# Retention: one written-out pipeline over all heads in place of a loop over head pairs

## The chip, the cores and the metric

The kernel runs on one core of one Trainium2 chip. The metric is the device time of one execution in microseconds (us), as the median of several runs. Engines are called PE (TensorE matmul), PEld (its weight loads, which overlap PE), DVE (VectorE), ACT (ScalarE), POOL (GpSimd) and SP (SyncE, which here only issues DMAs).

## What is computed

The kernel computes two layers of a decoder trunk on 1024 tokens of width 1024, all in float32. The change touches one stage of the second layer, the retention mixer, with 8 heads, key width 128, value width 256 and chunks of 128 tokens:

```python
def retention_mixer(h, positions, w_in, gn_g, gn_b, w_out):
    proj = h @ w_in                       # 1024 x (8*128 + 8*128 + 8*256 + 8*256)
    q, k, v, gate = jnp.split(proj, ...)
    q = apply_rope(q, cos, sin) * (RET_DK ** -0.5);  k = apply_rope(k, cos, sin)
    o = chunkwise_retention(q, k, v)
    o = layer_norm(o, gn_g, gn_b)         # per head
    return (jax.nn.silu(gate) * o) @ w_out
# chunkwise_retention, for each head and chunk i, with the head's decay powers:
#   inner = (q_i k_i^T * decay) v_i ;  cross = (q_i state) * cross_decay
#   state = state * chunk_decay + (k_i * key_decay)^T v_i
```

Heads are independent of one another. Within a head the chunks are chained by the state.

## The kernel before

`layer_1` runs its stages one after another, each in a block of its own that ends with a barrier of all engines: `modulate` (writes `g.hT`, the transposed input), `retention` (writes `mixT`), `mix_out` (the output projection) and then the mixture of experts.

In `retention` a step is one chunk of 128 tokens of one head. The weight panel of a head, `w[u]` (1024 rows by 768 columns, 3 MB), comes by four DMAs from SP (L1762). There are two such buffers, u = 0 and 1. A loop over `pairs` = 4 head pairs runs on every engine (`Fori`), and its body is 16 steps written out (`STEPS`): head 2m in `w[0]`, then head 2m+1 in `w[1]`.

The body is a software pipeline. In slot s PE issues, in this order, `project(s)` (q, k, v of the chunk: 8 matmuls of 512 columns, L1805), `output(s-2)` (L1834, L1836, L1837; without L1836 for the first chunk of a head), `turn(s-1)` (two transposes, L1821), `project_gate(s)` (8 matmuls of 256 columns, L1813), `score(s-1)` (L1827) and `turn_back(s-3)` (two transposes, L1844). A float32 matmul stands in the profile as two records. Since the body begins at s = 0 and runs to s = STEPS + 2, the pipeline is filled at the start of each pair and emptied at its end: slots 16, 17 and 18 of the body have only what is left of steps 13 to 15.

Behind PE, ACT takes q, k and v out of PSUM (`take`, L1879, L1881), makes the reciprocal root (`root`, L1894 and L1896, each with a table load), takes the turned q and k (`take_turned`, L1901), the gate (`take_gate`, L1888) and the turned result (`take_back`, L1907, into `mixT`). DVE ropes q and k (L1942 to L1947), masks the scores (L1952), updates the state, takes the moments (L1960 to L1966) and centres the output (L1971). POOL multiplies by the gain, adds the bias and multiplies by the gate (L1790, L1792, L1794); it reads `head_gain` and `head_bias`, copies of the pair's rows that it makes at the top of each pass (L1784, L1785).

All waits count from the start of the stage: `before(m, s)` and `after(m, s)` add `m * STEPS`, so inside the loop each wait compares a semaphore with a value worked out from the loop's register. SP waits at the top of pass m, for both panels, until all 16 gate projections of pass m-1 are done (`sp.wait_ge(S["gates"], m * STEPS)`).

Of the kernel before, what the change touches and what calls it, by code (L numbers as in the profile page):

```python
# [17 lines left out]
P = 128  # L18
D = 1024
T = 1024  # L20
NT = T // P
# [1681 lines left out]
def retention(g, mixT):  # L1703
    nc, io = g.nc, g.io
    STEPS = 2 * NT
# [4 lines left out]
    with ExitStack() as ctx:  # L1710
# [21 lines left out]
        head_gain = [sb(f"head_gain{u}", [P, RDV]) for u in range(2)]  # L1732
        head_bias = [sb(f"head_bias{u}", [P, RDV]) for u in range(2)]
# [6 lines left out]
        names = ("rows placed rates exps qkv gates taken gated roped turned turnc scored masked out moments logs roots norms rowsc "  # L1740
# [7 lines left out]
        for width in (RDK, RDK, RDV, RDV):  # L1748
            cols = w_dram[:, :, at:at + HEADS * width].rearrange("p k (m u n) -> p k m u n", u=2, n=width)
            parts.append((off, width, cols))  # L1750
            at += HEADS * width
            off += width
        pairs = HEADS // 2

        before = lambda m, s: m * STEPS + max(s, 0)
        after = lambda m, s: m * STEPS + s + 1

        @block.sync
        def _(sp):
            def panel(m, u):  # L1760
                for off, width, cols in parts:
                    sp.dma_start(w[u][:, :, off:off + width], cols[:, :, bass.ds(m, 1), u, :]  # L1762
                                 .rearrange("p k a n -> p k (a n)")).then_inc(w_in[u], 16)

            with sp.Fori(0, pairs) as m:
                for u in range(2):

                    sp.wait_ge(S["gates"], m * STEPS)
                    panel(m, u)

        @block.gpsimd
        def _(pool):
            pool.iota(place_i[:, :], [[1, 1]], base=1, channel_multiplier=1).then_inc(S["placed"], 1)
            for h in range(HEADS):
                pool.memset(rate[:, 0, h:h + 1], lg[h]).then_inc(S["placed"], 1)
                pool.memset(rate[:, 1, h:h + 1], -lg[h]).then_inc(S["placed"], 1)
                pool.memset(chunk_decay[:, h:h + 1], math.exp(RDK * lg[h])).then_inc(S["placed"], 1)
            pool.wait_ge(S["rows"], 32)
            gp = gain[:, :, :].rearrange("p (m u) n -> p m u n", u=2)
            bp = bias[:, :, :].rearrange("p (m u) n -> p m u n", u=2)  # L1780
            with pool.Fori(0, pairs) as m:
                for u in range(2):
                    row = lambda t: t[:, bass.ds(m, 1), u, :].rearrange("p a n -> p (a n)")
                    pool.tensor_copy(head_gain[u][:, :], row(gp)).then_inc(S["rowsc"], 1)  # L1784
                    pool.tensor_copy(head_bias[u][:, :], row(bp)).then_inc(S["rowsc"], 1)  # L1785
                for s in range(STEPS):
                    u, zb = s // NT, z[s % 4][:, :]
                    pool.wait_ge(S["norms"], after(m, s))
                    pool.wait_ge(S["rowsc"], m * 4 + 4)
                    pool.tensor_tensor(zb, zb, head_gain[u][:, :], ALU.mult).then_inc(S["gained"], 1)  # L1790
                    pool.wait_ge(S["gained"], m * 3 * STEPS + 3 * s + 1)
                    pool.tensor_tensor(zb, zb, head_bias[u][:, :], ALU.add).then_inc(S["gained"], 1)  # L1792
                    pool.wait_ge(S["gained"], m * 3 * STEPS + 3 * s + 2)
                    pool.tensor_tensor(zb, zb, gate[s % 4][:, :], ALU.mult).then_inc(S["gained"], 1)  # L1794

        @block.tensor
        def _(pe):
            with pe.Fori(0, pairs) as m:
                def project(s):
                    u, t = s // NT, s % NT  # L1800
                    if t == 0:
                        pe.wait_ge(w_in[u], m * 64 + 64)
                    pe.wait_ge(S["taken"], before(m, s - 1))
                    for kk in range(KD):
                        mm = pe.matmul(p_qkv[s % 2][:, :], g.hT[:, kk, t * P:(t + 1) * P], w[u][:, kk, 0:512],  # L1805
                                       start=(kk == 0), stop=(kk == KD - 1))
                    mm.then_inc(S["qkv"], 1)

                def project_gate(s):
                    u, t = s // NT, s % NT  # L1810
                    pe.wait_ge(S["gated"], before(m, s - 1))
                    for kk in range(KD):
                        mm = pe.matmul(p_gate[s % 2][:, 0:RDV], g.hT[:, kk, t * P:(t + 1) * P], w[u][:, kk, 512:W],  # L1813
                                       start=(kk == 0), stop=(kk == KD - 1))
                    mm.then_inc(S["gates"], 1)

                def turn(s):
                    pe.wait_ge(S["roped"], m * 6 * STEPS + 6 * s + 6)
                    pe.wait_ge(S["turnc"], before(m, s))
                    for i in range(2):  # L1820
                        mm = pe.transpose(p_turn[:, i * P:(i + 1) * P], qkr[s % 4][:, i, :], g.ident[:, :])  # L1821
                    mm.then_inc(S["turned"], 1)

                def score(s):
                    pe.wait_ge(S["turnc"], after(m, s))
                    pe.wait_ge(S["masked"], before(m, s))
                    pe.matmul(p_scores[:, 0:P], qkT[s % 2][:, 1, :], qkT[s % 2][:, 0, :], start=True, stop=True)\  # L1827
                        .then_inc(S["scored"], 1)

                def output(s):  # L1830
                    t = s % NT
                    pe.wait_ge(S["masked"], after(m, s))
                    pe.wait_ge(S["norms"], before(m, s))
                    pe.matmul(p_out[:, 0:RDV], scores[s % 2][:, :], v[s % 4][:, :], start=True, stop=(t == 0))  # L1834
                    if t:
                        pe.matmul(p_out[:, 0:RDV], qkT[s % 2][:, 0, :], state[(s - 1) % 2][:, :], start=False, stop=True)  # L1836
                    pe.matmul(p_out[:, RDV:2 * RDV], qkr[s % 4][:, 1, :], v[s % 4][:, :], start=True, stop=True)\  # L1837
                        .then_inc(S["out"], 1)

                def turn_back(s):  # L1840
                    pe.wait_ge(S["gained"], m * 3 * STEPS + 3 * s + 3)
                    pe.wait_ge(S["backc"], before(m, s))
                    for i in range(2):
                        mm = pe.transpose(p_back[:, i * P:(i + 1) * P], z[s % 4][:, i * P:(i + 1) * P], g.ident[:, :])  # L1844
                    mm.then_inc(S["back"], 1)

                for s in range(STEPS + 3):
                    if s < STEPS:
                        project(s)
                    if 0 <= s - 2 < STEPS:  # L1850
                        output(s - 2)
                    if 0 <= s - 1 < STEPS:
                        turn(s - 1)
                    if s < STEPS:
                        project_gate(s)
                    if 0 <= s - 1 < STEPS:
                        score(s - 1)
                    if 0 <= s - 3 < STEPS:
                        turn_back(s - 3)

        @block.scalar
        def _(act):
# [7 lines left out]
            dp = decay[:, :, :].rearrange("p i (m u) -> p i m u", u=2)  # L1870
            mp = mixT[:, :, :].rearrange("p (m k) t -> p m k t", k=4)
            with act.Fori(0, pairs) as m:
                def take(s):
                    u, b = s // NT, s % 4
                    act.wait_ge(S["qkv"], after(m, s))
                    act.wait_ge(S["roped"], m * 6 * STEPS + max(6 * (s - 1), 0))

                    act.wait_ge(S["out"], before(m, s - 3))
                    act.copy(v[b][:, :], p_qkv[s % 2][:, QK:512])  # L1879
                    for i in range(2):  # L1880
                        ins = act.activation(qk[s % 2][:, i, :], p_qkv[s % 2][:, i * RDK:(i + 1) * RDK], ACT.Copy,  # L1881
                                             scale=dp[:, i, bass.ds(m, 1), u])
                    ins.then_inc(S["taken"], 1)

                def take_gate(s):
                    act.wait_ge(S["gates"], after(m, s))
                    act.wait_ge(S["gained"], m * 3 * STEPS + max(3 * (s - 3), 0))
                    act.activation(gate[s % 4][:, :], p_gate[s % 2][:, 0:RDV], ACT.Silu).then_inc(S["gated"], 1)  # L1888

                def root(s):  # L1890
# [791 lines left out]
```

## Time and profile before

| | |
|---|---|
| median of 3 runs | 3802.49 us |
| lowest and highest of them | 3797.62, 3807.16 us |
| the profiled execution | 3790.52 us |
| its span, first to last instruction | 3788.7 us |
| PE busy over the span | 3229.5 us (85%) |
| ACT, DVE, POOL busy | 24%, 34%, 13% |
| retention, first projection to last transpose | 1923.52 to 2770.99 us of the span |

A timeline row has the start, the duration, the engine, the line, the operation with its output and inputs, the count of merged records, and in brackets how long the engine sat idle before it and what ended that. Ends of matmuls are modelled and overlap a little, so durations on PE are best read as the distance between the starts of two rows. A row of windows gives for a stretch its length, then for each engine the busy us and the number of instructions, then the granted TensorE clock as a share of full speed, the DMA share and GB/s.

### The profile page before, as it was taken

How to read it: one execution, taken by the hardware profiler on the slowest of the kernel's cores; microseconds unless marked ns; L12 is line 12 of the kernel's file. 1: busy time of each engine (PE TensorE's matmuls, PEld its weight loads, DVE VectorE, ACT ScalarE, POOL GpSimd, SP SyncE). 2: the span in 40 equal slices, each digit the busy share in tenths (PEclk: the TensorE clock that was granted, in tenths of full speed). 3: DMA queues.
4: the chain of work that ended last, by engine and by line, in shares of the span. 5: the costliest groups of instructions: out<-in, count | busy, mean ns of one | idle time of the engine just before them, and what ended most of it. 6: DMA issues, size and time to landing. Idle time of an engine off the chain costs nothing. (4 is left out here: it accounts for less than half of the span.)

```text
span 3788.7 us, 44646 instructions
## 1 busy us (share of the span) xinstructions
PE 3229.5 (85%) x15035; PEld 1782.1 (47%) x15036; DVE 1274.6 (34%) x3073; ACT 908.2 (24%) x1749; POOL 503.7 (13%) x866
## 2 busy tenths in 40 slices
PE   7978889677865999999479899999989759988884
PEld 5656654367434434333146565655644343433331
DVE  4665554354243112221623232232311241121226
ACT  1022224123120111111135354453410011111111
POOL 0000010166010000000301111111100100000003
PEclk9879999778885999999689999999989859999997
DMA  7722001122235999996530202010030157899985
GB/s 283 270 87 84 0 23 34 49 65 47 89 104 230 388 367 411 425 426 236 214 111 1 67 0 67 0 45 22 0 122 34 60 230 300 329 427 424 426 358 200
DMA packets 195570, 668.26 MB, mean 176 GB/s; under 512 B 46863, under 2 KB 97770, under 8 KB 162414
## 3 DMA queue, kind: packets, MB, share of 16 engines
q1 hardware_dynamic: 162574, 579.56, 39.5%
q0 software_dynamic: 14144, 51.39, 3.5%
q10 hardware_dynamic: 18720, 35.66, 2.5%
q8 instruction: 70, 1.15, 0.1%
q14 instruction: 62, 0.51, 0.0%
HBM read 605.17 MB, written 61.37 MB: 176 GB/s over the span
## 5 line engine op out<-in xcount | busy, mean ns | idle before, releaser
L1805 PE MATMUL ret_pqkv<-ret_w,hT_mix 128*128 128x512 f32 x1024 | 457.6, 600 | 20.0 <-DMA ret_w<-in_ret_w_in_dram 20.0
L2354 PE MATMUL f0e_pgu<-f0w_gu,f0e_xT 128*64 128x512 f32 x1568 | 344.8, 596 | 7.0 <-issue 3.2
L1678 PE MATMUL mo_py<-mo_w,mixT 128*128 128x512 f32 x768 | 333.4, 597 | 4.8 <-DMA mo_w<-in_ret_w_out_dram 2.5
L1805 PEld LDWEIGHTS ret_pqkv<-ret_w,hT_mix 128*128 128x128 f32 x1024 | 192.6, 193 | 240.1 <-issue 239.9
L2354 PE MATMUL f1e_pgu<-f1w_gu,f1e_xT 128*64 128x512 f32 x1344 | 296.0, 595 | 7.4 <-issue 3.6
L1678 PEld LDWEIGHTS mo_py<-mo_w,mixT 128*128 128x128 f32 x768 | 147.0, 192 | 192.6 <-issue 184.8
L1813 PE MATMUL ret_pgate<-ret_w,hT_mix 128*128 128x256 f32 x1024 | 231.6, 379 | 0.0
L2354 PEld LDWEIGHTS f0e_pgu<-f0w_gu,f0e_xT 128*64 128x64 f32 x1568 | 125.4, 138 | 220.9 <-issue 220.8
L2373 PE MATMUL f1e_pd<-f1w_d,f1e_hidT 128*64 128x512 f32 x672 | 173.1, 668 | 52.6 <-DMA f1w_d<-in_moe_w_down_dram 51.3
L1813 PEld LDWEIGHTS ret_pgate<-ret_w,hT_mix 128*128 128x128 f32 x1024 | 189.9, 190 | 25.0 <-issue 1.9
L2354 PEld LDWEIGHTS f1e_pgu<-f1w_gu,f1e_xT 128*64 128x64 f32 x1344 | 104.2, 138 | 194.1 <-issue 194.0
L2373 PE MATMUL f0e_pd<-f0w_d,f0e_hidT 128*64 128x512 f32 x784 | 176.9, 600 | 7.4 <-DMA f0w_d<-in_moe_w_down_dram 5.5
L434 PE MATMUL gc_pq<-hT_mix,gc_w 128*128 128x512 f32 x384 | 168.3, 597 | 10.1 <-DMA gc_w<-in_hy_w_in_dram 10.1
L1960 DVE TENSOR_TENSOR ret_state<-ret_state,ret_pout 128x256 f32<-128x256 f32 x56 | 23.5, 421 | 406.2 <-PE ret_pout L1837 406.2
L2502 DVE COPY f0e_hidT<-f0e_ph 128x512 f32<-128x512 f32 x32 | 22.1, 691 | 363.7 <-PE f0e_ph L2366 363.3
L2502 DVE COPY f1e_hidT<-f1e_ph 128x512 f32<-128x512 f32 x32 | 22.1, 691 | 359.0 <-PE f1e_ph L2366 359.0
L1790 POOL TENSOR_TENSOR ret_z<-ret_z,ret_head_gain 128x256 f32<-128x256 f32 x64 | 46.5, 726 | 700.5 <-DVE ret_z L1971 700.5
L2373 PEld LDWEIGHTS f1e_pd<-f1w_d,f1e_hidT 128*64 128x64 f32 x672 | 53.0, 153 | 149.4 <-issue 93.5
L434 PEld LDWEIGHTS gc_pq<-hT_mix,gc_w 128*128 128x128 f32 x384 | 73.4, 192 | 102.3 <-issue 91.9
L1879 ACT COPY ret_v<-ret_pqkv 128x256 f32<-128x256 f32 x64 | 23.8, 372 | 389.1 <-PE ret_pqkv L1805 389.1
L1598 DVE TENSOR_TENSOR mo_z<-mo_py,mo_gate_b 128x1024 f32<-128x1024 f32 x16 | 19.6, 1225 | 272.0 <-PE mo_py L1678 272.0
L2373 PEld LDWEIGHTS f0e_pd<-f0w_d,f0e_hidT 128*64 128x64 f32 x784 | 58.3, 138 | 102.7 <-issue 94.2
(547 smaller groups left out, 4705.4 us busy)
## 6 DMA issues: line engine op xcount, KB each, us to landing
f0w_gu<-in_moe_w_gate_dram SPq DMA_DIRECT2D x32, 2048.0 KB, 11.3
f0w_gu<-in_moe_w_up_dram SPq DMA_DIRECT2D x32, 2048.0 KB, 16.8
f0w_d<-in_moe_w_down_dram SPq DMA_DIRECT2D x64, 1024.0 KB, 15.8
f1w_gu<-in_moe_w_gate_dram SPq DMA_DIRECT2D x32, 2048.0 KB, 25.5
f1w_gu<-in_moe_w_up_dram SPq DMA_DIRECT2D x32, 2048.0 KB, 30.5
f1w_d<-in_moe_w_down_dram SPq DMA_DIRECT2D x64, 1024.0 KB, 24.9
mixT<-in_ada_w_dram SPq DMA_DIRECT2D x80, 512.0 KB, 5.6
expert_rows<-f0e_y ACTq DMA_DIRECT2D x64, 256.0 KB, 10.4
```

The lines of the kernel that those rows point to most:

```text
L434: mm = pe.matmul(pq[u][:, half * 512:(half + 1) * 512], w[u][:, kk, :], g.hT[:, kk, half * 512:(half + 1) * 512], start=(kk == 0), stop=(k ...
L1598: dve.tensor_tensor(z[:, :], y, self.gate_b[:, :], ALU.mult).then_inc(S["zmul"], 1)
L1678: mm = pe.matmul(py[t % 3][:, half * 512:(half + 1) * 512], mixT[:, kk, t * P:(t + 1) * P], ws[:, kk, half * 512:(half + 1) * 512], start= ...
L1790: pool.tensor_tensor(zb, zb, head_gain[u][:, :], ALU.mult).then_inc(S["gained"], 1)
L1805: mm = pe.matmul(p_qkv[s % 2][:, :], g.hT[:, kk, t * P:(t + 1) * P], w[u][:, kk, 0:512], start=(kk == 0), stop=(kk == KD - 1))
L1813: mm = pe.matmul(p_gate[s % 2][:, 0:RDV], g.hT[:, kk, t * P:(t + 1) * P], w[u][:, kk, 512:W], start=(kk == 0), stop=(kk == KD - 1))
L1879: act.copy(v[b][:, :], p_qkv[s % 2][:, QK:512])
L1960: ch.mark(dve.tensor_tensor(st[:, :], state[(s - 1) % 2][:, :], p_out[:, RDV:2 * RDV], ALU.add))
L2354: mm = pe.matmul(pgu[s][half * HALF:(half + 1) * HALF, :], xT[u % 2][:, kk, s * HALF:(s + 1) * HALF], ew.gu[u][:, :, kk, half * FH:(half + ...
L2373: mm = pe.matmul(pd[s][half * HALF:(half + 1) * HALF, :], hidT[:, s, k % 2, k // 2, :], ew.d[u % 2][:, k, half * DH:(half + 1) * DH], star ...
L2502: dve.tensor_copy(hidT[:, :, :, :, :].rearrange("p s j h t -> p (s j h t)"), ph[:, :])\
```

## The change

The loop over pairs is gone on all engines. `STEPS` is now 64, all eight heads, written out once; the pipeline is filled at step 0 of head 0 and emptied after step 63. Every wait compares with a constant. Head h uses `w[h % 2]`. SP loads the panel of head h as soon as the gates of head h-2 are done, the head that had the same buffer. `head_gain` and `head_bias`, their copies and the semaphore `rowsc` are gone, POOL reads `gain[:, h, :]` and `bias[:, h, :]`. The order of the operations within a slot, the number of buffers and all operations on PE, ACT and DVE stay as they are.

```diff
-    STEPS = 2 * NT
+    STEPS = HEADS * NT
...
-        head_gain = [sb(f"head_gain{u}", [P, RDV]) for u in range(2)]
-        head_bias = [sb(f"head_bias{u}", [P, RDV]) for u in range(2)]
...
-        before = lambda m, s: m * STEPS + max(s, 0)
-        after = lambda m, s: m * STEPS + s + 1
+        before = lambda s: max(s, 0)
+        after = lambda s: s + 1
...
-            with sp.Fori(0, pairs) as m:
-                for u in range(2):
-
-                    sp.wait_ge(S["gates"], m * STEPS)
-                    panel(m, u)
+            for h in range(HEADS):
+                if h >= 2:
+                    sp.wait_ge(S["gates"], (h - 1) * NT)
                 for off, width, cols in parts:
+                    sp.dma_start(w[h % 2][:, :, off:off + width], cols[:, :, h, :]).then_inc(w_in[h % 2], 16)
...
-            with pool.Fori(0, pairs) as m:
-                for u in range(2):
-                    row = lambda t: t[:, bass.ds(m, 1), u, :].rearrange("p a n -> p (a n)")
-                    pool.tensor_copy(head_gain[u][:, :], row(gp)).then_inc(S["rowsc"], 1)
-                    pool.tensor_copy(head_bias[u][:, :], row(bp)).then_inc(S["rowsc"], 1)
-                for s in range(STEPS):
-                    pool.wait_ge(S["rowsc"], m * 4 + 4)
-                    pool.tensor_tensor(zb, zb, head_gain[u][:, :], ALU.mult).then_inc(S["gained"], 1)
+            for s in range(STEPS):
+                h, zb = s // NT, z[s % 4][:, :]
+                pool.tensor_tensor(zb, zb, gain[:, h, :], ALU.mult).then_inc(S["gained"], 1)
...
-            with pe.Fori(0, pairs) as m:
-                def project(s):
-                    u, t = s // NT, s % NT
-                    if t == 0:
-                        pe.wait_ge(w_in[u], m * 64 + 64)
-                    pe.wait_ge(S["taken"], before(m, s - 1))
+            def project(s):
+                h, t = s // NT, s % NT
+                if t == 0:
+                    pe.wait_ge(w_in[h % 2], 64 * (h // 2 + 1))
+                pe.wait_ge(S["taken"], before(s - 1))
...
```

The other functions of the five engines change in the same way: `before(m, s)` to `before(s)`, slices by `bass.ds(m, 1)` to slices by h.

## Rows read from the trace of the kernel before

**Rows 1.** PE timeline: the first projection of each of the four passes
```profile
1923.52 9.16 PE L1805 MATMUL ret_pqkv<-ret_w,hT_mix 128*128 128x512 f32 x16 [20.04 <-DMA ret_w<-in_ret_w_in_dram]
...
2135.67 8.90 PE L1805 MATMUL ret_pqkv<-ret_w,hT_mix 128*128 128x512 f32 x16
...
2347.46 4.96 PE L1805 MATMUL ret_pqkv<-ret_w,hT_mix 128*128 128x512 f32 x7
...
2559.17 5.34 PE L1805 MATMUL ret_pqkv<-ret_w,hT_mix 128*128 128x512 f32 x8
```

**Rows 2.** Windows: steps 3 to 14 of passes 0 and 1
```profile
1958.60:2107.10 148.50, 148.50 (x528) 92.64 (x527) 45.25 (x157) 72.44 (x132) 26.27 (x37) 1.00 0.00 1
2170.49:2319.01 148.52, 148.52 (x529) 92.64 (x527) 45.30 (x158) 72.46 (x132) 26.28 (x37) 1.00 0.00 0
```

**Rows 3.** Windows: step 10, with a head's first output, and step 11
```profile
2045.41:2057.50 12.09, 12.09 (x45) 7.37 (x44) 3.86 (x14) 6.19 (x12) 2.09 (x4) 1.00 0.01 2
2057.50:2069.90 12.40, 12.40 (x47) 7.75 (x45) 3.77 (x14) 5.94 (x12) 2.26 (x4) 1.00 0.00 1
```

**Rows 4.** PE timeline: the end of pass 0, from output(14) on
```profile
2119.84 0.70 PE L1834 MATMUL ret_pout<-ret_v,ret_scores 128*128 128x256 f32 x2 [0.17 <-DVE ret_scores L1952]
...
2124.93 0.49 PE L1827 MATMUL ret_pscores<-ret_qkT 128*128 128x128 f32 x2 [3.31 <-ACT ret_qkT L1901]
...
2125.80 1.22 PE L1834 MATMUL ret_pout<-ret_v,ret_scores 128*128 128x256 f32 x2 [0.16 <-DVE ret_scores L1952]
...
2134.98 0.69 PE L1844 MATMUL ret_pback<-ident,ret_z 128*128 128x128 f32 x2 [5.83 <-POOL ret_z L1794]
```

**Rows 5.** PE timeline: the end of pass 3
```profile
2755.10 0.70 PE L1834 MATMUL ret_pout<-ret_v,ret_scores 128*128 128x256 f32 x2 [0.17 <-DVE ret_scores L1952]
...
2770.30 0.69 PE L1844 MATMUL ret_pback<-ident,ret_z 128*128 128x128 f32 x2 [6.04 <-POOL ret_z L1794]
2774.89 3.78 PE L1572 MATMUL mo_py<-mo_diag,ones 128*128 128x512 f32 x4 [3.89 <-DVE mo_diag L1565]
```

**Rows 6.** Windows: the gap between passes 0 and 1
```profile
2119.84:2135.67 15.83, 6.53 (x22) 4.40 (x23) 4.09 (x13) 8.13 (x14) 6.80 (x12) 0.79 1.05 308
```

**Rows 7.** SP timeline: the panel loads at the start and after pass 0
```profile
1906.62 18.45 SPq L1762 DMA_DIRECT2D ret_w<-in_ret_w_in_dram  x8
...
2119.27 14.55 SPq L1762 DMA_DIRECT2D ret_w<-in_ret_w_in_dram  x8
```

**Rows 8.** DMA view, 2131 to 2152: GB/s in 40 equal slices of 0.525 us
```profile
GB/s 295 295 287 295 287 311 342 345 363 332 312 343 353 351 355 334 205 74 59 6 0 0 0 0 0 0 0 0 0 0 0 0 0 0 0 0 0 0 0 0
```

**Rows 9.** ACT timeline: `take_back` under a panel load, and in the steady part
```profile
2125.76 0.37 ACT L1907 COPY mixT<-ret_pback 128x256 f32 x1 [0.88 <-PE ret_pback L1844]
...
2246.18 0.37 ACT L1907 COPY mixT<-ret_pback 128x256 f32 x1
```

**Rows 10.** DMA view, passes 0 (1923 to 2134) and 1 (2152 to 2346): instruction queues
```profile
q8 instruction: 6, 0.10, 0.2%
q14 instruction: 5, 0.04, 0.1%
...
q14 instruction: 3, 0.02, 0.0%
```

**Rows 11.** Windows: the longest stretch at full granted clock, in the experts
```profile
1231.90:1576.64 344.74, 337.37 (x1638) 137.87 (x1636) 63.99 (x152) 53.38 (x133) 21.86 (x38) 1.00 0.96 395
```

**Rows 12.** PE timeline: gate, and what follows the score, in step 1 and steadily
```profile
2154.95 3.62 PE L1813 MATMUL ret_pgate<-ret_w,hT_mix 128*128 128x256 f32 x16
...
2158.62 1.88 PE L1805 MATMUL ret_pqkv<-ret_w,hT_mix 128*128 128x512 f32 x4
...
2253.29 3.62 PE L1813 MATMUL ret_pgate<-ret_w,hT_mix 128*128 128x256 f32 x16
...
2257.09 0.38 PE L1844 MATMUL ret_pback<-ident,ret_z 128*128 128x128 f32 x2
```

More of the change, by code:

```diff
@@ L1739, in retention @@
         p_back = g.ps(ctx, "ret_pback", [P, 512])
-        names = ("rows placed rates exps qkv gates taken gated roped turned turnc scored masked out moments logs roots norms rowsc "
+        names = ("rows placed rates exps qkv gates taken gated roped turned turnc scored masked out moments logs roots norms "
                  "gained back backc").split()
@@ L1748, in retention @@
         for width in (RDK, RDK, RDV, RDV):
[L1749 removed]
+            cols = w_dram[:, :, at:at + HEADS * width].rearrange("p k (h n) -> p k h n", n=width)
             parts.append((off, width, cols))
@@ L1796, in _ @@
         @block.tensor
         def _(pe):
-            with pe.Fori(0, pairs) as m:
-                def project(s):
-                    u, t = s // NT, s % NT
-                    if t == 0:
-                        pe.wait_ge(w_in[u], m * 64 + 64)
-                    pe.wait_ge(S["taken"], before(m, s - 1))
[L1804 to L1859, printed above, removed]
@@ new lines, in project, with project_gate @@
+            def project(s):
[3 more added lines that the diff above has]
+                pe.wait_ge(S["taken"], before(s - 1))
+                for kk in range(KD):
+                    mm = pe.matmul(p_qkv[s % 2][:, :], g.hT[:, kk, t * P:(t + 1) * P], w[h % 2][:, kk, 0:512],
+                                   start=(kk == 0), stop=(kk == KD - 1))
+                mm.then_inc(S["qkv"], 1)
+            def project_gate(s):
+                h, t = s // NT, s % NT
+                pe.wait_ge(S["gated"], before(s - 1))
+                for kk in range(KD):
+                    mm = pe.matmul(p_gate[s % 2][:, 0:RDV], g.hT[:, kk, t * P:(t + 1) * P], w[h % 2][:, kk, 512:W],
+                                   start=(kk == 0), stop=(kk == KD - 1))
+                mm.then_inc(S["gates"], 1)
@@ new lines, in turn, with score @@
+            def turn(s):
+                pe.wait_ge(S["roped"], 6 * s + 6)
+                pe.wait_ge(S["turnc"], before(s))
+                for i in range(2):
+                    mm = pe.transpose(p_turn[:, i * P:(i + 1) * P], qkr[s % 4][:, i, :], g.ident[:, :])
+                mm.then_inc(S["turned"], 1)
+            def score(s):
+                pe.wait_ge(S["turnc"], after(s))
+                pe.wait_ge(S["masked"], before(s))
+                pe.matmul(p_scores[:, 0:P], qkT[s % 2][:, 1, :], qkT[s % 2][:, 0, :], start=True, stop=True)\
+                    .then_inc(S["scored"], 1)
@@ new lines, in output @@
+            def output(s):
+                t = s % NT
+                pe.wait_ge(S["masked"], after(s))
+                pe.wait_ge(S["norms"], before(s))
+                pe.matmul(p_out[:, 0:RDV], scores[s % 2][:, :], v[s % 4][:, :], start=True, stop=(t == 0))
+                if t:
+                    pe.matmul(p_out[:, 0:RDV], qkT[s % 2][:, 0, :], state[(s - 1) % 2][:, :], start=False, stop=True)
+                pe.matmul(p_out[:, RDV:2 * RDV], qkr[s % 4][:, 1, :], v[s % 4][:, :], start=True, stop=True)\
+                    .then_inc(S["out"], 1)
@@ new lines, in turn_back @@
+            def turn_back(s):
+                pe.wait_ge(S["gained"], 3 * s + 3)
+                pe.wait_ge(S["backc"], before(s))
+                for i in range(2):
+                    mm = pe.transpose(p_back[:, i * P:(i + 1) * P], z[s % 4][:, i * P:(i + 1) * P], g.ident[:, :])
+                mm.then_inc(S["back"], 1)
+            for s in range(STEPS + 3):
+                if s < STEPS:
+                    project(s)
+                if 0 <= s - 2 < STEPS:
+                    output(s - 2)
+                if 0 <= s - 1 < STEPS:
+                    turn(s - 1)
+                if s < STEPS:
+                    project_gate(s)
+                if 0 <= s - 1 < STEPS:
+                    score(s - 1)
+                if 0 <= s - 3 < STEPS:
+                    turn_back(s - 3)
@@ new lines, in take @@
+            def take(s):
+                h, b = s // NT, s % 4
+                act.wait_ge(S["qkv"], after(s))
+                act.wait_ge(S["roped"], max(6 * (s - 1), 0))
+                act.wait_ge(S["out"], before(s - 3))
+                act.copy(v[b][:, :], p_qkv[s % 2][:, QK:512])
+                for i in range(2):
+                    ins = act.activation(qk[s % 2][:, i, :], p_qkv[s % 2][:, i * RDK:(i + 1) * RDK], ACT.Copy,
+                                         scale=decay[:, i, h:h + 1])
+                ins.then_inc(S["taken"], 1)
@@ new lines, in take_gate, with root @@
+            def take_gate(s):
+                act.wait_ge(S["gates"], after(s))
+                act.wait_ge(S["gained"], max(3 * (s - 3), 0))
+                act.activation(gate[s % 4][:, :], p_gate[s % 2][:, 0:RDV], ACT.Silu).then_inc(S["gated"], 1)
+            def root(s):
+                act.wait_ge(S["moments"], 5 * s + 5)
+                act.wait_ge(S["norms"], before(s - 1))
+                act.activation(rstd[s % 2][:, :], mv[s % 2][:, 1:2], ACT.Ln).then_inc(S["logs"], 1)
+                act.wait_ge(S["logs"], after(s))
+                act.activation(rstd[s % 2][:, :], rstd[s % 2][:, :], ACT.Exp, scale=-0.5).then_inc(S["roots"], 1)
@@ new lines, in take_turned, with take_back @@
+            def take_turned(s):
+                act.wait_ge(S["turned"], after(s))
+                act.wait_ge(S["out"], before(s - 1))
+                act.copy(qkT[s % 2][:, :, :].rearrange("p a t -> p (a t)"), p_turn[:, 0:2 * P])\
+                    .then_inc(S["turnc"], 1)
+            def take_back(s):
+                h, t = s // NT, s % NT
+                act.wait_ge(S["back"], after(s))
+                act.copy(mixT[:, 2 * h:2 * h + 2, t * P:(t + 1) * P],
+                         p_back[:, 0:2 * P].rearrange("p (k t) -> p k t", k=2)).then_inc(S["backc"], 1)
@@ L1922, in _ @@
+            for s in range(STEPS + 3):
+                if s < STEPS:
+                    take(s)
+                if 0 <= s - 2 < STEPS:
+                    root(s - 2)
+                if 0 <= s - 1 < STEPS:
+                    take_turned(s - 1)
+                if s < STEPS:
+                    take_gate(s)
+                if 0 <= s - 3 < STEPS:
+                    take_back(s - 3)
         @block.vector
@@ new lines, in centre @@
+            def centre(s):
+                dve.wait_ge(S["roots"], after(s))
+                dve.wait_ge(S["back"], before(s - 3))
+                dve.tensor_scalar(z[s % 4][:, :], p_out[:, 0:RDV], mv[s % 2][:, 0:1], rstd[s % 2][:, 0:1],
+                                  ALU.subtract, ALU.mult).then_inc(S["norms"], 1)
+            for s in range(STEPS + 2):
+                if 0 <= s - 2 < STEPS:
+                    finish(s - 2)
+                if s < STEPS:
+                    rope(s)
+                if 0 <= s - 2 < STEPS:
+                    centre(s - 2)
+                if 0 <= s - 1 < STEPS:
+                    mask(s - 1)
```

141 lines of the change are left out of this document (37 added, 104 removed).

## The prediction

> **What bounds the kernel now.** The stages are separated by barriers, so only the retention stage can change, and every microsecond that it loses or gains reaches the end. I read the PE timeline first, for where each pass of the loop begins: 1923.52, 2135.67, 2347.46 and 2559.17 [rows 1]. A pass takes 212.15, 211.79 and 211.71 us; the last ends at 2770.30 + 0.69 = 2770.99 [rows 5], 211.82 us after its start. Then I looked into a pass. In steps 3 to 14 PE is busy for all of 148.50 us, at a granted clock of 1.00, and the next pass repeats this within 0.02 us [rows 2]. One step is 12.40 us, the one with a head's first output 12.09 [rows 3]; 11 x 12.40 + 12.09 = 148.49 gives the 148.50 back. So in the steady part PE is the bound, by its columns alone, and no register arithmetic, wait or fetch shows.
>
> Between passes it isn't. From the 2119.84 of output(14) to the next pass's first projection 15.83 us go by, of which PE is busy 6.53 [rows 6]. The row by row view shows why: the emptying pipeline is a chain with nothing to put in between. PE waits 3.31 us for ACT's turned q and k, then 5.83 us for POOL's last product, which itself follows ACT's two table loads and DVE's centring [rows 4]. After the wait the clock is low too: output(15) takes 1.22 us as drawn against 0.70 for output(14), the same two records [rows 4], and the next pass's first projection 8.90 us as drawn [rows 1]. The granted clock over the gap is 0.79, so the lower of its two levels (1.2 and 2.4 GHz) in part of it [rows 6]. The panel load isn't what PE waits for: it was issued at 2119.27 [rows 7] and the POOL wait ended last.
>
> **The change part by part.** *Fill and drain go, three times.* In the after, step 16 follows step 15 as step 9 follows step 8. A crossing of heads inside the written-out body is already in every pass, at step 8, and lies within the 148.50 us [rows 2], so it costs nothing besides the 0.31 us that a first output saves. From output(14) of pass 0 (2119.84, [rows 4]) to its counterpart of the last pass (2755.10, [rows 5]) are 635.26 us. The after has 48 steps there, 6 of them with a first output (heads 2 to 7): 42 x 12.40 + 6 x 12.09 = 593.3 us. The difference is 41.9 us, 14.0 for each of three gaps. It can be split: PE idle 15.83 - 6.53 = 9.3 us, and the rest, about 4.7, is the lower clock in the drain and in the first projection. What precedes step 15 of pass 0 and what follows the last output stays: the first load (PE idle 20.04 us, [rows 1]), one fill, one drain, 3.9 us to the next stage's first matmul [rows 5].
>
> *Panels one head earlier.* The load of head h is now released by the gates of head h-2 and needed when head h begins, 8 steps or 98.9 us later. At the start of the stage the panel of head 0 went from issue at 1906.62 to PE's start at 1923.52, 16.9 us [rows 1, 7], while a second panel and two more tables were being issued. That leaves some 82 us of slack; the cover is whole. Nothing but panels is queued on SP in this stage, so a waiting SP holds up nobody. If the cover were gone, the price would be up to 16.9 us at each of 6 heads.
>
> *Loads beside full compute.* Before, the loads ran mostly in the gap; now each 3 MB comes under steady steps. The nearest rows: while both panels came in at 308 GB/s in the gap [rows 6], ACT's copy at 2125.76 took 0.37 us, as at 2246.18 with no load [rows 9]. In the experts PE stays at 337.37 of 344.74 us busy with the DMA share at 0.96 [rows 11]. I take nothing. The other bound: ACT has no slack in a steady step. The gate's first matmul is 3.80 us ahead of what follows the score in a steady step, 3.67 in step 1, where the score doesn't wait for ACT's copy [rows 12]. So if a load slowed ACT, PE would feel it. Two panels took from 2119.27 to about 2141.5, 22 us, until the queue ran dry [rows 7, 8], so one load spans at most two steps; I bound it at 1 us a step, 12 steps, 12 us lost.
>
> *Constants instead of registers, no loop.* Since PE is gapless in the steady part, there is nothing to gain on it, except that 0.13 us (3.80 - 3.67) by which the score comes late. If ACT became quicker by as much, 61 steps would give 7.9 us. ACT's order and instructions stay the same, and the DVE and ACT work ahead of that copy are chained by data, so I take 0 and keep 7.9 for the lower end. Entry and exit of the loops lie under the first load and under the drain: nothing to 0.5 us, taken as 0.
>
> *POOL's copies.* They fall in POOL's idle time at the top of a pass, POOL being busy 6.80 us even in the gap [rows 6]; their removal is worth 0, and could cost nothing, as the operands are of the same shape.
>
> *A longer instruction stream.* Pass 0 fetched 6 blocks of 16 KB on one instruction queue and 5 small ones on the other, pass 1 fetched none on the first and 3 on the second [rows 10]. So the first queue, which I read as PE's, since it alone has that much to fetch, kept the body between passes; written out, it has to fetch some 18 blocks more. The price of a fetched block follows from [rows 2]: pass 0 with its fetches took 148.50 us for the 12 steps, pass 1 without took 148.52. That is 0. The Trainium skill says of this (Runtime: NRT & Kernel Launch, section Instruction fetch mechanics) that blocks in sequence are fetched ahead and mostly hidden, whereas a taken branch out of the pages held makes the engine wait. Its first half agrees with the trace and lowers the chance that I give to a fetch-bound PE. By its second half each loop end would carry a stall; none shows on PE, whose last transpose at 2134.98 is followed by the projection 0.69 us later [rows 1, 4], and by that sentence the sum would be unchanged, since any such stall lies within the pass times above.
>
> *The sum.* 41.9 us off the profiled execution: 3790.52 to 3748.6, span 3788.7 to 3746.8. The timed runs lie 12 us above the profiled one; what is taken away is a fixed piece, so I subtract it from the median: 3802.49 - 41.9 = 3760.6 us.
>
> **The rivals.** (1) *ACT gets quicker*, the 0.13 us goes: 3752.7. For it: the wait shows in every steady step [rows 12]. Against: nothing of its work is removed.
>
> (2) *Loads under full compute cost up to 12 us*: 3772.6. For it: ACT has no slack. Against: [rows 9, 11].
>
> (3) *The clock doesn't hold.* PE would be busy without a pause for about 790 us, where it now gets a rest every 200. If full clock were granted only for a time, half clock would cost half of its duration: the gain is used up after 84 us at the lower level, and beyond it the kernel is slower; with a tenth more (92 us) it would stand at about 3807. Against: the full level was granted through 344.74 us with PE 98% busy [rows 11], and the steps of [rows 2] show no sign of slowing.
>
> (4) *PE becomes bound by its instruction stream.* Place: PE, steps 16 to 63. It decides when each of the 18 extra blocks stalls PE by over 2.3 us (41.9 / 18). A block that meets a panel load could wait for it, up to the 14.55 us in which two panels are issued [rows 7]; if all 18 did so half of that, 7.3 us, it would be 131 us lost, 3892. But loads run for about 6 x 10 of 600 us, so two blocks would meet one: 15 us, 3775. Against: [rows 2, 10].
>
> (5) *The change doesn't do what it says*: PE waits for a panel at each head, 6 x 16.9 = 101 us more: 3862. It would need a load of over 98.9 us.
>
> **How the numbers follow.** The forecast has 0.80, rival 1 0.05, rival 2 0.07, rival 3 0.03, rival 4 0.04 (mostly its small form), rival 5 0.01. The measurement of this kernel can tell about 0.3%, 11.4 us, from no change; the forecast and rivals 1 and 2 are all beyond it, the small form of 4 as well. So faster 0.95, same 0.02, slower 0.03. The range takes in 3752.7 and 3772.6, and on either side something for the spread of the runs (about 5 us around their median) and for the 12 us between profiled and timed: 3747 to 3775.
>
> **What would show it.** In the profile after: the distance between projections 12.40 us through steps 16, 32 and 48, and 12.09 for a head's second step after its first; PE idle on "POOL ret_z" once, not four times (5.8 to 6.0 us each); granted clock 1.00 in every window from step 3 to step 63; six separate loads of four DMAs each, about 99 us apart; from the first projection to the last transpose 805.6 us instead of 847.5; more blocks on the first instruction queue. Wrong would be: steps longer than 12.40 in the first two steps of heads 1 to 6 (rival 2), a lower clock late in the stage (3), idle PE with "issue" every 35 us (4), or PE waiting for ret_w (5).

## The result, and the profile after

| | before | after |
|---|---|---|
| median, same chip and rounds (4 and 4 runs) | 3802.76 us | 3755.89 us |
| lowest and highest | 3797.62, 3807.16 | 3749.89, 3758.68 |
| ratio, 95% interval | | 0.9875 (0.9858 to 0.9892) |
| the profiled execution, its span | 3790.52, 3788.7 | 3749.89, 3748.2 |
| retention, first projection to last transpose | 847.47 | 803.68 |

The forecast was 3760.6 us; the kernel takes 3755.9, inside the range of 3747 to 3775. In a second comparison of five rounds (below) the same kernel stands at 0.9905 (0.9888 to 0.9921), so the two comparisons give 46.9 and 37.9 us. The retention stages of the two profiles differ by 43.8 us, which lies between these two, and the changed kernel's stage came out within 0.15 us when it was profiled again (803.68, 803.54). The stage is therefore the sharper measure, and I use it for everything below, with one reserve: its very first step and its last drain vary by about 1.5 and 1.2 us between profiles of kernels that do the same work there, so a difference of a microsecond or two between two stages is read from the distances between projections.

What answers to [rows 1], [rows 4] and [rows 5]: the PE timeline of the changed kernel, at the first projection, around step 16, where the gap between pairs 0 and 1 was, and at the end.

```profile
1927.36 8.64 PE L1787 MATMUL ret_pqkv<-ret_w,hT_mix 128*128 128x512 f32 x16 [21.04 <-DMA ret_w<-in_ret_w_in_dram]
...
2118.61 3.62 PE L1795 MATMUL ret_pgate<-ret_w,hT_mix 128*128 128x256 f32 x16
2122.08 0.49 PE L1809 MATMUL ret_pscores<-ret_qkT 128*128 128x128 f32 x2
2122.41 0.38 PE L1826 MATMUL ret_pback<-ident,ret_z 128*128 128x128 f32 x2
2122.63 7.03 PE L1787 MATMUL ret_pqkv<-ret_w,hT_mix 128*128 128x512 f32 x16
2129.49 0.59 PE L1816 MATMUL ret_pout<-ret_v,ret_scores 128*128 128x256 f32 x2
...
2715.76 0.70 PE L1816 MATMUL ret_pout<-ret_v,ret_scores 128*128 128x256 f32 x2 [0.17 <-DVE ret_scores L1929]
...
2730.35 0.69 PE L1826 MATMUL ret_pback<-ident,ret_z 128*128 128x128 f32 x2 [5.82 <-POOL ret_z L1777]
```

Here and below, a gap is the stretch from the last projection of one pass to the first of the next, and a drain is the emptying of the pipeline in it. At 2122.63 step 16 begins 0.22 us after the transposes of step 13, with a projection of 7.03 us as drawn against 8.90 in [rows 1], and with no bracket for idle time. The one wait for POOL that is left is the one at the end. The windows of the changed kernel (columns as in [rows 2]) show the whole stretch from step 3 to the end of step 63, a step under which a panel comes in, the one after it, and a step with a head's first output:

```profile
1961.81:2715.42 753.61, 753.61 (x2672) 470.09 (x2670) 225.41 (x794) 369.61 (x671) 132.85 (x184) 1.00 0.09 26
2023.82:2036.23 12.41, 12.41 (x46) 7.76 (x45) 3.70 (x14) 6.07 (x12) 2.19 (x4) 1.00 0.84 255
2036.23:2048.63 12.40, 12.40 (x46) 7.75 (x45) 3.69 (x14) 6.05 (x12) 2.17 (x4) 1.00 0.00 0
...
2147.43:2159.41 11.98, 11.98 (x45) 7.38 (x44) 3.70 (x14) 6.07 (x12) 2.18 (x4) 1.00 0.00 0
```

PE is busy for all of 753.61 us at a granted clock of 1.00. The step with a DMA share of 0.84 takes 12.41 us, the one without 12.40. The DMA view of the changed kernel from 1923 to 2720 shows the loads, where there were pairs of them in the gaps: the rest of the first two, then six of their own, about 99 us apart.

```profile
GB/s 205 1 0 1 0 159 1 0 1 1 159 0 1 1 1 159 0 1 1 6 154 0 1 0 18 142 0 1 0 32 128 1 1 0 1 0 1 0 1 0
...
q8 instruction: 22, 0.36, 0.2%
```

### The profile page after: what moved, and what is told of

The parts are those of the page before. It is cut to its first block and busy times, and to the rows that moved or that the text cites. A ratio compares the mean times of both kernels' runs of the same rounds, so it can differ in the third digit from the quotient of the medians.

```text
span 3748.2 us, 43330 instructions
## 1 busy us (share of the span) xinstructions
PE 3215.4 (86%) x15035; PEld 1777.2 (47%) x15036; DVE 1272.4 (34%) x3073; ACT 910.7 (24%) x1752; POOL 497.3 (13%) x850
## 5 line engine op out<-in xcount | busy, mean ns | idle before, releaser
L1773 POOL TENSOR_TENSOR ret_z<-ret_z,ret_gain 128x256 f32<-128x256 f32 x64 | 46.5, 726 | 670.8 <-DVE ret_z L1948 670.8
## 6 DMA issues: line engine op xcount, KB each, us to landing
f0w_gu<-in_moe_w_gate_dram SPq DMA_DIRECT2D x32, 2048.0 KB, 13.8
```

The lines of the kernel that those rows point to most:

```text
L1773: pool.tensor_tensor(zb, zb, gain[:, h, :], ALU.mult).then_inc(S["gained"], 1)
```

## The experiments

Ten more runs were made. Lengths are from the first projection of the stage to its last transpose, ratios are to the kernel before in the same rounds, with 95% intervals. The intervals of the last four rows overlap one another, so what these edits are worth is read from the stage.

| kernel | stage, us | ratio |
|---|---|---|
| before | 847.47 | 1 |
| changed | 803.68 | 0.9875 (0.9858 to 0.9892) |
| changed, again | 803.54 | 0.9905 (0.9888 to 0.9921) |
| two passes, one gap | 817.90 | 0.9918 (0.9893 to 0.9943) |
| four passes, three gaps | 845.35 | 1.0003 (0.9994 to 1.0013) |
| eight passes, seven gaps | 901.09 | 1.0141 (1.0122 to 1.0160) |
| panels loaded late | 846.63 | 0.9988 (0.9976 to 1.0001) |
| four passes, PE kept busy in the drains | 834.09 | 0.9983 (0.9969 to 0.9996) |
| panels released one step ahead | 806.10 | 0.9891 (0.9869 to 0.9913) |
| ACT's order exchanged | 795.53 | 0.9874 (0.9852 to 0.9896) |
| the same, gain and bias later | 797.91 | 0.9868 (0.9845 to 0.9891) |
| the same, PE kept busy in its waits | 793.93 | 0.9863 (0.9847 to 0.9880) |

**The gaps by their number.** The order in which the five engines' steps are written is nested, with everything else as in the changed kernel, constants and early loads included. `GS`, the steps of a pass, is 8, 16 or 32:

```diff
-            for s in range(STEPS + 3):
-                if s < STEPS:
-                    project(s)
+            for o in range(0, STEPS, GS):
+                for s in range(GS + 3):
+                    if s < GS:
+                        project(o + s)
```

> The changed kernel, written out with constants and early panel loads, but the pipeline emptied and filled again after every 16 steps, as in the kernel before: four passes, three gaps. Theory A (the whole gain is the three gaps): the same time as the kernel before, 3803 us, three gaps of about 15.8 us between output(14) and the next pass's first projection, ratio 0.998 to 1.002. Theory B (constants instead of registers, no branches, or the early loads bring part of it): faster than before by that part; if it were the 5 us by which the measured gain (46.9) exceeds the forecast (41.9), 3798 us.

> The same with eight passes of one head each: seven gaps instead of three. Theory A: each gap costs 14.0 us wherever it stands, so 4 x 14.0 = 56 us over four passes and 98 us over the changed kernel: 3854 us, ratio 1.014. Theory B makes the same difference to four passes but from a lower start. If a second mechanism limits (the panel of the next head not there in time, since SP waits for the gates of the head before last), PE would be seen waiting for ret_w in the gaps.

> The same with two passes of four heads: one gap. Theory A: 14.0 us over the changed kernel, 3770 us, ratio 0.991. With this run, four points (0, 1, 3 and 7 gaps) should lie on a line of 14.0 us a gap. Rival (a clock that holds only for a time under full load): one gap would cost less than 14.0, since its rest would give something back.

Against the 803.68 us of no gap, the stage is 14.2 us longer with one gap, 41.7 with three (13.9 each) and 97.4 with seven (13.9 each). Not all of that stands in the gaps: 1.2 us of the first figure and 1.4 of the second are the very first step (13.12 and 13.35 against 11.93 us), and about 0.5 us of each is the last drain. From the last projection of a pass to the fourth of the next, less 3 x 12.40 + 11.97 us for the same steps without a gap, the one gap costs 12.4 us, the three cost 12.3, 13.7 and 13.8, and the seven 13.8 to 13.9 each. PE's idle time is 9.4 to 9.5 us in every one of them, so the two cheap ones, the only gap of two passes and the first of four, are cheap by their clock. The expected 14.0 us holds within 0.4 for the other nine. The dense steps take 12.40 or 12.41 us in all four kernels, however far the last gap is, so the clock gives nothing back for a rest. Theory B is worth little: four passes written out with constants and with early loads take 845.35 us in the stage and the loop 847.47. The ratio of 1.0003 says the same. In none of the three does PE wait for a panel after the start of the stage. Of the 2.1 us, 0.9 stand in eight steps (some 0.12 us each, see the point on the sum further down); the rest is the clock's: 2.1 us less in the gaps, 0.9 more in the very first step. Loop, registers and load times by themselves bring about 2 us; overlap across the pairs is what brings the gain.

**Early panels as a condition.** One line of SP's wait in the changed kernel:

```diff
-                    sp.wait_ge(S["gates"], (h - 1) * NT)
+                    sp.wait_ge(S["gates"], h // 2 * 2 * NT)
```

> The changed kernel, but both panels of a pair are loaded when the gates of the pair before are done, as before. Theory A with its second half (crossing the pairs is worth something only because the panels come earlier): at the start of heads 2, 4 and 6 PE has only output, turn, score and turn_back to do, about 2 us, and then waits for a panel that took 16.9 to 18.2 us at the start of the stage and 3 MB at about 300 GB/s, 10 us, in the gap: 9 to 15 us of idle PE each, plus the low clock behind it, 3 x 11 to 3 x 17. So 3789 to 3807 us; in the trace PE waits three times for ret_w. Rival (the panels come in time anyway and the gaps were the pipeline's alone): 3756 us, the time of the changed kernel.

The stage takes 846.63 us: the gain is gone almost to the last microsecond, with another cause in the gap's place. PE timeline of this kernel at step 16:

```profile
2120.46 0.38 PE L1826 MATMUL ret_pback<-ident,ret_z 128*128 128x128 f32 x2
2132.14 9.47 PE L1787 MATMUL ret_pqkv<-ret_w,hT_mix 128*128 128x512 f32 x16 [11.30 <-DMA ret_w<-in_ret_w_in_dram]
```

PE waits 11.30 us for the panel, and the projection behind it runs in part at the lower clock (9.47 us as drawn against 7.03). The list of waits has 55.4 us on ret_w in four, 20.4 of them at the start of the stage. So the two halves of the change are worth next to nothing alone. Written out without the early loads it gains 0.8 us in the stage, and the early loads with four separate passes 2.1.

**How early.** The same line with one step of lead instead of eight:

```diff
-                    sp.wait_ge(S["gates"], (h - 1) * NT)
+                    sp.wait_ge(S["gates"], (h - 1) * NT + 7)
```

> The changed kernel, but SP releases each panel only one step (12.4 us) before it is needed instead of eight. It measures the load's own time under full compute and the slack of 82 us. By the forecast a panel takes 10 us (3 MB at 300 GB/s) to 16.9 us (start of the stage), so PE waits 0 to 5 us for ret_w at each of heads 2 to 7, at most 27 us in all: 3750 to 3778 us on the scale of the first comparison, steps of 12.40 us otherwise. The run with the late loads showed 11.3 us of waiting where 0 steps of lead were left and 2 us of matmuls; that gives 11.3 + 1.5 - 12.4, about 0.5 us a head. Rival (loads under full compute are slower than in a gap): 5 us or more a head.

The list of waits of PE has nothing on ret_w after the start. The stage is 2.4 us longer than that of the changed kernel: 1.2 of it lie in its very first step (13.14 us between starts against 11.93, before any panel is released), 0.85 in the last drain, and 0.4 in four steps at the ends and starts of heads, steps 40, 48, 55 and 56, which take 12.47 to 12.51 us. That is where the lead just runs out: from SP's first issue to the landing of the last part the six panels take 12.5 to 12.8 us, and they land 0.04 to 0.25 us before the projection that needs them. At head 7 the weight load shows the wait:

```profile
2616.14 0.30 PEld L1787 LDWEIGHTS ret_pqkv<-ret_w,hT_mix 128*128 128x128 f32 x2 [0.17 <-DMA ret_w<-in_ret_w_in_dram]
```

So a panel of 3 MB under full compute takes up to 12.8 us, and the slack with eight steps of lead was about 86 us, more than the 82 of the forecast. With PE idle, in the run before, the first panel of a pair took 11.8 to 12.4 us from issue to PE's start; loads under full compute are slower than that by a microsecond at most. The 16.9 us that I had taken is what the start of the stage costs, where gain and bias share the queues (shown below).

**What a gap consists of.** Matmuls of constants, extra work, are put into the waits of each drain, in four passes:

```diff
+            def spin(t, n):
+                for _ in range(n):
+                    pe.matmul(t[:, P:2 * P], g.ident[:, :], g.ones[:, :], start=True, stop=True)
...
+                    if s == GS:
+                        spin(p_scores, 14)
                     if 0 <= s - 1 < GS:
                         score(o + s - 1)
+                    if s == GS + 2:
+                        spin(p_scores, 26)
```

> Four written-out passes (three gaps) as in the run of four passes, but PE multiplies in the waits of the drain: 14 matmuls of 128 columns (about 3.0 us at full clock) where it waited 3.31 us for ACT's turned q and k, 26 (about 5.6 us) where it waited 5.8 to 6.0 us for POOL's last product; they write a part of a PSUM bank that nobody reads. It splits a gap into wait and clock. By the forecast a gap is 9.3 us of idle and 4.7 us of lower clock: 3 x 4.7 = 14 us less than the run of four passes, ratio about 0.997 to the kernel before, and the next pass's first projection 7.03 us as drawn instead of 8.2 to 8.9. Rival (the clock part is small, the gap is all idle): no change against four passes, ratio 1.000.

The stage is 11.3 us shorter than four plain passes, where 14 were expected. PE timeline of this kernel from the last output of the first pass on:

```profile
2131.11 0.70 PE L1817 MATMUL ret_pout<-ret_v,ret_scores 128*128 128x256 f32 x2 [0.16 <-DVE ret_scores L1940]
...
2133.25 5.97 PE L1832 MATMUL ret_pscores<-ones,ident 128*128 128x128 f32 x52
2139.05 0.38 PE L1827 MATMUL ret_pback<-ident,ret_z 128*128 128x128 f32 x2
2139.27 7.03 PE L1788 MATMUL ret_pqkv<-ret_w,hT_mix 128*128 128x512 f32 x16
```

The output takes 0.70 us as drawn where [rows 4] has 1.22, and the projection 7.03 where [rows 1] has 8.90. The product of POOL that the last transposes need was ready at 2138.88, so the added matmuls, which end as those begin, held nothing up. The distances between projections price the clock: from the last projection of a pass to the next pass's first, and from there to its second, are 26.85 + 10.33 = 37.2 us with PE kept busy in all three gaps. The kernel before has 28.57 + 12.19, 28.45 + 12.11 and 28.47 + 12.07, so the lower clock cost 3.6, 3.4 and 3.4 us a gap. The four plain passes have 27.48 + 11.51, 28.40 + 11.92 and 28.36 + 12.13: 1.8, 3.1 and 3.3 us. That makes 8.3 us of the 11.3; 1.4 are the very first step, which is the same code in both (13.35 against 11.91 us), and the rest is the last drain.

**ACT's part in a steady step.** Two lines change places:

```diff
+                if 0 <= s - 1 < STEPS:
+                    take_turned(s - 1)
                 if 0 <= s - 2 < STEPS:
                     root(s - 2)
-                if 0 <= s - 1 < STEPS:
-                    take_turned(s - 1)
```

> The changed kernel with one exchange in ACT's order within a slot: the copy of the turned q and k before the reciprocal root with its two table loads. Rival 1 of the forecast (the score waits for ACT, 0.13 us a step): steps of 12.27 instead of 12.40 us, 61 x 0.13 = 8 us less in the stage. Against it: the gate's activation and the root then come 0.35 us later, and the centred output with them; by the timeline they have over 5 us of slack, so nothing. If the 0.13 us is PE's own (a weight load that can't be taken ahead of the score's wait), the steps stay at 12.40 us.

The steps are 12.28 us instead of 12.40 (11.85 instead of 11.97), and the stage is 8.15 us shorter, as expected; about 7.7 of that are the steps. In the changed kernel ACT's copy stood behind two table loads; ACT timeline of the changed kernel, then ACT and PE timeline with the exchange:

```profile
2031.81 1.28 ACT L1873 ACT_TABLE_LOAD   x1
...
2033.88 1.28 ACT L1875 ACT_TABLE_LOAD   x1
2035.17 0.20 ACT L1875 ACTIVATE ret_rstd<-ret_rstd 128x1 f32<-128x1 f32 x1
2035.28 0.35 ACT L1880 COPY ret_qkT<-ret_pturn 128x256 f32<-128x256 f32 x1
```

```profile
2245.43 3.62 PE L1795 MATMUL ret_pgate<-ret_w,hT_mix 128*128 128x256 f32 x16
2245.64 0.37 ACT L1880 COPY ret_qkT<-ret_pturn 128x256 f32<-128x256 f32 x1 [0.62 <-PE ret_pturn L1803]
...
2248.89 0.39 PE L1809 MATMUL ret_pscores<-ret_qkT 128*128 128x128 f32 x2
```

The copy now ends 2.9 us before the score, while the gate's matmuls still run, and the score follows them without a break. Rival 1 of the prediction named the right wait and price; the change doesn't touch it in a dense step.

**The start of the stage.** The loads of gain and bias move behind ACT's first `take`:

```diff
-            act.dma_start(gain[:, :, :].rearrange("p h n -> p (h n)"), io["ret_gn_g"][0].partition_broadcast(P))\
-                .then_inc(S["rows"], 16)
-            act.dma_start(bias[:, :, :].rearrange("p h n -> p (h n)"), io["ret_gn_b"][0].partition_broadcast(P))\
-                .then_inc(S["rows"], 16)
...
                 if s < STEPS:
                     take(s)
+                if s == 0:
+                    act.dma_start(gain[:, :, :].rearrange("p h n -> p (h n)"), io["ret_gn_g"][0].partition_broadcast(P))\
+                        .then_inc(S["rows"], 16)
+                    act.dma_start(bias[:, :, :].rearrange("p h n -> p (h n)"), io["ret_gn_b"][0].partition_broadcast(P))\
+                        .then_inc(S["rows"], 16)
```

> The exchange of the run before, and the loads of gain and bias (2 x 1 MB) issued after the first take instead of at the stage's start, where they share the queues with the first panel. If they hold up the first panel: PE's wait for ret_w at the stage's start (20 to 21 us) falls by the time of 2 MB at 300 GB/s, at most 7 us, likely 3 to 5. If SP's issuing sets the panel's arrival (8 DMAs in 18.45 us): nothing. POOL needs the rows some 25 us later, enough for 2 MB.

PE's wait for the first panel falls from 21.3 to 15.5 us, by 5.8. From SP's first issue (1915.11 in both) to the last transpose it is 810.7 us against 814.0: 3.4 are kept. The first step took longer this time, 13.10 us against 11.81, as it does from run to run (below), and the last drain 1.1 us longer, which also makes the length in the table longer.

Last, with both edits kept, the matmuls of constants in PE's waits, `spin` as above:

```diff
+            spin(p_scores, 56)
             for s in range(STEPS + 3):
...
+                if s == STEPS:
+                    spin(p_scores, 14)
                 if 0 <= s - 1 < STEPS:
                     score(s - 1)
+                if s == STEPS + 2:
+                    spin(p_scores, 26)
                 if 0 <= s - 3 < STEPS:
                     turn_back(s - 3)
```

> The changed kernel with both edits of the run before (ACT's exchange, gain and bias later) and with PE kept busy where it waits: 56 matmuls of 128 columns before the first projection (PE waits 15.5 us there for the first panel), 14 and 26 in the one drain that is left, into a part of a PSUM bank that nobody reads. If the lower clock after a wait is what costs 3.75 us a gap (the run with work in three gaps), the first projection takes 6.9 instead of 8.2 to 9.7 us between starts (1.3 to 2.7 us less) and the drain about 2 us less: the stage 3 to 5 us shorter than the 797.9 us of the run before, 793 to 795 from first projection to last transpose. Against the kernel before: 847.5 - 794 = 53 us in the stage and 5 at its start, ratio 0.984 to 0.986. Rival: the matmuls delay the first projection or are themselves at the low clock for most of the wait, and nothing is left: 797 to 798.

The first step takes 10.32 us, 2.8 less, and the stage 793.93 us, as expected. But the 56 matmuls ran partly at the lower clock and ended late: they took 15.24 us as drawn, and the projection began 15.1 us after SP's first issue instead of 12.7. From that issue to the last transpose it is 809.1 us, 1.6 less than without them, so the rival of this expectation was half right. In the same rounds it stands at 0.9863 (0.9847 to 0.9880) and the changed kernel at 0.9905 (0.9888 to 0.9921), intervals apart. Counted from SP's first issue, the changed kernel takes 821.6 us there and this one 809.1; most of these 12.5 us come from ACT's order and the later rows.

**The changed kernel again**, without any edit, in the rounds of the run before:

> The changed kernel as it is, on the same chip and in the same rounds, to tell what lies between 41.9 us (forecast), 43.8 us (its retention stage in the two profiles) and 46.9 us (the medians). If the gain is the stage alone, 43.8 us or a ratio of 0.9885, with an interval that excludes neither 41.9 nor 46.9 by much; if something outside the stage changed, a ratio at or below 0.9875.

The second measurement of the changed kernel gives 37.9 us by the medians. Together with the first, 46.9, it surrounds the 43.8 of the stage. As a ratio 43.8 us are 0.9885, inside the first interval and just outside the second, and the 41.9 us of the forecast, 0.9890, lie in both; nothing points to a gain outside the stage. What moves between runs is ahead of the stage: its first projection began at 1923.5 to 1937.1 us in the twelve profiles, almost all of it in code that the kernels share, while what follows the last transpose took 1014.9 to 1020.6 us.

## Why the prediction was right, point by point

*PE bound by its columns alone in the steady part, 12.40 us a step*: the step is right, through all eight heads, and no fetch or register shows in it. But 0.12 us of it is the score's wait for ACT, as the exchange shows (12.28 us), though PE is drawn busy all through; the prediction had this as 0.13 further on, and it didn't change the sum.

*The sum, 41.9 us for three gaps*: right, in its mechanism and nearly in its size. Removing three gaps from the same written-out code is worth 41.7 us in the stage, 39.8 of them in the gaps themselves; that it meets 41.9 so closely is in part the luck of a slow very first step in that run. In the kernel before, the distances between projections put the three gaps at 14.1, 13.9 and 13.9 us, and in the changed kernel all of this is gone. The stage fell by 43.8 against a forecast of 41.9, from 847.5 to 803.7 instead of 805.6. The missing 1.9 us can be found in the distances between projections: the seven steps with a head's first output take 11.97 instead of 12.09 (0.8 us), the first filled step is 0.1 shorter, the very first step 11.93 instead of 12.45 (0.5), the last drain 0.6. The last two vary from run to run; the first is a real small gain of the new code, which I had put at nothing under *Constants instead of registers*, and the four passes have it too. The rows place it on DVE, in the step with a head's first output (step 10, which begins at 2045.41 before and at 2048.63 after):

```profile
2054.26 0.35 DVE L1964 TENSOR_SCALAR ret_state<-ret_state,ret_chunk_decay 128x256 f32<-128x256 f32 x1 [0.15 <-DVE ret_stats L1963]
```

```profile
2057.37 0.35 DVE L1941 TENSOR_SCALAR ret_state<-ret_state,ret_chunk_decay 128x256 f32<-128x256 f32 x1
```

The state's decay began 8.85 us into the step and now begins at 8.74, with no bracket before it, and what hangs on it follows as much earlier: ACT's copy of the turned q and k, and the score, at 11.43 instead of 11.54 us. In the kernel before, this instruction takes its factor by the loop's register and waits for a semaphore value worked out from it; now both are constants. That this is the cause is likely but not shown: in a dense step of the kernel before, the same instruction follows without a bracket.

*The split of a gap*: the idle time of 9.3 us was right. The term of 4.7 us for the lower clock was too large: 3.4 to 3.6 us are the clock's in the kernel before, as the run with matmuls in the drains shows. With PE at full speed all through, a gap still costs 10.5 us over the steady steps (26.85 + 10.33 + 10.76 less 3 x 12.40, less the 0.22 of transposes that the next slot lacks), and that is 1.0 to 1.2 more than the idle time of a gap. A small part can be read: an output after a wait is drawn with 0.70 us, one in sequence with 0.59. The rest isn't isolated. I had taken the remainder of a subtraction and given it one name.

*The panels*: right that the cover is whole, too cautious on the price. A load under compute needs 12.8 us at most in the six of that run, not 16.9.

*Loads under full compute at nothing, bound 12 us*: the zero was right, 12.41 against 12.40 us, with eight steps of lead. Rival 2 is out.

*The stream of instructions*: the first queue moved 87 blocks over the whole execution instead of 70, 17 more where I had said some 18, and the dense steps, 12.40 us in both kernels, show no price for them. The page's sentence on blocks in sequence (the Trainium skill, Runtime: NRT & Kernel Launch, section Instruction fetch mechanics) agrees with this. Its other sentence, a stall for taken branches, still has no row here: four written-out passes and the loop differ by 2.1 us over three branches, and the distances place that elsewhere: 1.8 us in the lower clock of one gap, 0.3 in that of the other two, 0.12 on each of eight steps, less 0.9 by which the very first step was longer. Rival 4 is out.

*The clock under a long load*: 753.61 us at 1.00, and the dense steps stay at 12.40 or 12.41 us with no gap, one, three or seven. Rival 3 is out.

*The median*: 46.9 and 37.9 us in two comparisons around a forecast of 41.9. Subtracting a fixed piece was sound; the rest is spread that arises ahead of the stage.

## What to carry to other kernels

Price a loop boundary by the distance from the last dense step of one pass to the first dense step of the next, less the same work at the dense rate; here that gave 13.9 to 14.1 us a gap in the kernel before and 12.3 to 13.9 in the written-out passes, without knowing what the gap consists of. An overlap across a boundary brings its gain only when the data for the far side are there (without the early panels 0.8 us of 43.8 were left): look for the load that the boundary used to hide, and release it by the last reader of its buffer rather than by the end of the pass. When an engine's order puts two table loads ahead of a copy that PE waits for, look at the order first: the exchange of two lines brought 8.15 us here, a fifth of what the rewrite brought.

## What I hadn't expected of the hardware

The same 9.4 to 9.5 us of idle PE cost 1.8, 3.1 and 3.3 us of lower clock in one execution of one kernel (four passes), and 3.6, 3.4 and 3.4 in the kernel before. The very first step after the long wait took 11.8 to 13.4 us in eleven profiles of the same work on PE. A microsecond or two on a stage with a wait in it is thus no sign of the change. And 3 MB at 255 GB/s beside full compute left no mark on a pipeline without slack: 12.41 against 12.40 us.
